# Two-stream diffusion step: the entering states of the backward scan copied by ScalarE in all four groups, not by GpSimd in three

## The reference, cut to what matters

```python
bu = einsum("blgc,gpc->blgp", u, b_bar)          # real and imaginary part
h[l] = a_bar * h[l-1] + bu[l]                    # forward, and on the reversed tokens
y = einsum(h_fwd, c_fwd) + einsum(h_bwd, c_bwd)[reversed] + d_skip * u
y = gelu(y); y = y * sigmoid(y @ w_glu + b_glu)
out = (y * silu(z)) @ w_out ;  x = x + gate * out
```

## Time and profile before

| | us |
|---|---|
| median of 3 runs (lowest, highest) | 1102.53 (1101.49, 1105.61) |
| time of the profiled execution | 1102.69 |
| its span | 1100.9 |
| granted clock of TensorE, mean | 0.992 |
| TensorE matmuls busy | 1054.0 (96%) |
| VectorE busy | 766.8 (70%) |
| ScalarE busy | 538.3 (49%) |
| GpSimd busy | 227.3 (21%) |
| all 284 grouped low-part subtractions (L1557) | 347.9 |
| all 284 grouped high-part roundings (L1152) | 299.2 |

### The profile page before, as it was taken

How to read it: one execution, slowest core, us unless ns; L and a number is a source line. 1 busy time by engine, 2 the same in 40 slices (tenths; PEclk the granted TensorE clock), 3 DMA queues, 4 the chain that set the end, 5 groups by cost and what they waited for, 6 DMA issues and landing times.

```text
span 1100.9 us, 18580 instructions
## 1 busy us (share of the span) xinstructions
PE 1054.0 (96%) x7426; PEld 823.8 (75%) x7426; DVE 766.8 (70%) x1206; ACT 538.3 (49%) x759; POOL 227.3 (21%) x382
## 2 busy tenths in 40 slices
PE   3999999999999999999999989999999989999996
PEld 2777777777777777777777768888788868878885
DVE  2765686766577667766688876369998996476564
ACT  5334454444434344444444465566657466454442
POOL 1111230432043403321233340200222322100000
PEclk9999999999999999999999999999999999999999
DMA  9999978999789979997799987968684958865552
GB/s 378 419 419 419 380 285 317 359 347 350 289 318 356 361 276 344 340 354 262 286 369 348 349 317 261 286 220 251 185 268 156 297 186 290 299 237 173 187 197 93
DMA packets 62407, 325.61 MB, mean 296 GB/s; under 512 B 8209, under 2 KB 14993, under 8 KB 30193
## 3 DMA queue, kind: packets, MB, share of 16 engines
q1 hardware_dynamic: 42944, 267.93, 65.4%
q0 software_dynamic: 12176, 45.33, 11.9%
q10 hardware_dynamic: 7200, 11.16, 2.8%
HBM read 296.04 MB, written 28.34 MB: 295 GB/s over the span
## 4 chain that ended last, share of the span: by engine, by line
PE 75%; DVE 10%; DMA 7%; ACT 4%; issue 2%; SPq 0%; POOL 0%; ACTq 0%; DVEq 0%
PE ps L867 20%; PE ps L869 19%; PE ps L868 19%; DMA raw<-in_w 5%; PE ps L732 5%; DVE wlo L1557 3%; DMA early<-in_wada 2%; DVE sb L1685 2%; PE ps L991 2%; PE ps L806 1%; ACT whi L1152 1%; PE ps L1015 1%; PE ps L789 1%; DVE t L1680 1%; PE ps L751 1%
## 5 line engine op out<-in xcount | busy, mean ns | idle before, releaser
L1557 DVE TENSOR_TENSOR wlo<-raw,whi 128x1024 fp32r<-128x1024 f32 x284 | 347.9, 1228 | 232.6 <-ACT whi L1152 227.8
L1152 ACT ACTIVATE whi<-raw 128x1024 fp32r<-128x1024 f32 x284 | 299.2, 1058 | 397.6 <-PE ps L869 373.5
L867 PE MATMUL ps<-whi,xhi 128*128 128x512 f32 x1136 | 460.5, 405 | 9.7 <-DVE wlo L1557 6.6
L868 PE MATMUL ps<-wlo,xhi 128*128 128x512 f32 x1152 | 451.2, 392 | 0.0
L869 PE MATMUL ps<-whi,xlo 128*128 128x512 f32 x1136 | 445.2, 392 | 0.0
L867 PEld LDWEIGHTS ps<-whi,xhi 128*128 128x128 f32 x1136 | 214.1, 188 | 83.7 <-issue 18.9
L869 PEld LDWEIGHTS ps<-whi,xlo 128*128 128x128 f32 x1136 | 214.1, 188 | 47.2
L868 PEld LDWEIGHTS ps<-wlo,xhi 128*128 128x128 f32 x1152 | 217.5, 189 | 41.0
L732 PE MATMUL ps<-araw,cT 128*32 128x512 f32 x496 | 59.4, 596 | 0.0
L1685 DVE TENSOR_TENSOR sb<-sb,t 128x128 f32<-128x128 f32 x140 | 48.4, 349 | 4.6
L1575 DVE TENSOR_TENSOR xlo<-ps,xhi 128x512 fp32r<-128x512 f32 x40 | 27.5, 689 | 16.9 <-ACT xhi L1173 16.6
(11 more groups left out here) (236 smaller groups left out, 1066.2 us busy)
## 6 DMA issues: line engine op xcount, KB each, us to landing
raw<-in_w SPq DMA_DIRECT2D x144, 1024.0 KB, 7.0
araw<-in_wadag SPq DMA_DIRECT2D x62, 1024.0 KB, 9.0
early<-in_wada SPq DMA_DIRECT2D x20, 1024.0 KB, 19.0
araw<-in_wada SPq DMA_DIRECT2D x12, 1024.0 KB, 17.6
btab_scratch<-bs ACTq DMA_DIRECT2D x32, 256.0 KB, 6.2
ctab_scratch<-ce POOLq DMA_DIRECT2D x16, 512.0 KB, 8.6
btab<-btab_scratch SPq DMA_DIRECT2D x16, 512.0 KB, 4.6
ctab<-ctab_scratch POOLq DMA_DIRECT2D x16, 512.0 KB, 4.7
```

Of the source, the lines that this page charges most:

```text
L867: mm(acc, xhi[:, kt, st], hi[:, k], start=kt == 0, stop=False)
L868: mm(acc, xhi[:, kt, st], wlo[:, slot, k0 % 2, k], start=False, stop=False)
L1152: af(whi_at(k).rearrange("p k c -> p (k c)"), src, ACT.Copy).then_inc(s_hi, 1)
L1557: tt(wlo[:, slot, k % 2].rearrange("p k c -> p (k c)"), src, whi_at(k).rearrange("p k c -> p (k c)").bitcast(F32), ALU.subtract).then_inc( ...
```

## The change

For the groups 0, 1 and 2 the backward half of the entering states is copied by ScalarE, as it already is for group 3. GpSimd's function goes, with its waits, and so does the semaphore `s_hyb` that TensorE, ScalarE and GpSimd waited for.

```diff
-            def entering_backward(w):
-                pool.wait_ge(s_scan, w + 1)
-                if w == 0:
-                    pool.wait_ge(s_h0, 16)
-                for q in range(4):
-                    if (w, q) == (0, 2):
-                        pool.wait_ge(s_uT, 2 * NW)
-                        pool.wait_ge(s_u2p, 2 * NW)
-                    if w >= 1:
-                        pool.wait_ge(s_y, 4 * w + q - 3)
-                    pool.wait_ge(s_wused, HY_AT[w] + q + 1)
-                    dst, first, src = entering(w, q)
-                    nc.gpsimd.tensor_copy(dst[S5P:P, :, :, NCH - 1], first[S5P:P])
-                    nc.gpsimd.tensor_copy(dst[S5P:P, :, :, 0:NCH - 1], src[S5P:P, :, :, ::-1]).then_inc(s_hyb, 1)
...
-            entering_backward(0)
-            entering_backward(1)
-            entering_backward(2)
-            pool.wait_ge(s_hyb, 12)
...
                 pe.wait_ge(s_hy, n + 1)
-                pe.wait_ge(s_hyb, min(n + 1, 4 * (NW - 1)))
...
                     act.wait_ge(s_hy, 4 * (w - 2) + q + 1)
-                    act.wait_ge(s_hyb, 4 * (w - 2) + q + 1)
...
                 af(fwd[:, :, :, 0], first[0:S5P], ACT.Copy)
-                if w == NW - 1:
-                    af(bwd[:, :, :, NCH - 1], first[S5P:P], ACT.Copy)
-                    nc.scalar.copy(bwd[:, :, :, 0:NCH - 1], src[S5P:P, :, :, ::-1])
+                if n == 0:
+                    act.wait_ge(s_h0, 16)
+                af(bwd[:, :, :, NCH - 1], first[S5P:P], ACT.Copy)
+                nc.scalar.copy(bwd[:, :, :, 0:NCH - 1], src[S5P:P, :, :, ::-1])
                 nc.scalar.copy(fwd[:, :, :, 1:NCH], src[0:S5P]).then_inc(s_hy, 1)
```

More of the change, by code:

```diff
@@ L389, in build @@
         s_S, s_Ssb = sem("S_pe"), sem("S_sb")
-        s_scan, s_hy, s_hyb, s_y, s_ysb = sem("scan"), sem("hy"), sem("hy_backward"), sem("y_pe"), sem("y_sb")
+        s_scan, s_hy, s_y, s_ysb = sem("scan"), sem("hy"), sem("y_pe"), sem("y_sb")
         s_yout, s_yin = sem("y_stored"), [sem(f"y_in{i}") for i in range(NW)]
```

## The result

The changed kernel takes 1106.74 us in the median of 20 runs (1104.47 to 1114.73), the kernel before 1102.49: 4.3 us slower by the medians. The ratio of the means is 1.0043, with a 95% interval of 1.0034 to 1.0051, or +4.7 us; a run of the kernel before that took 1184.40 us is not in it. That is clearly slower, and not quite the 0.5% that the prediction took as the line for a change. Forecast were 1104.5 us and "the same". The profiled execution of the changed kernel is its fastest one: 1104.47 us, span 1102.2, against 1102.69 and 1100.9 of the one before. Of the 4.3 us it shows only 1.8.

A forecast was written before the change was run, and what follows sets the result against it. TensorE, busy 96%, was taken to bound the kernel, with ScalarE and VectorE as possible limits beside it. Delays less VectorE's gain came to +1.8, taken as +2.0 us: 1104.7 on the profiled execution, 1104.5 forecast, range 1102 to 1107.

The forecast's parts named there:

- GpSimd's side costs nothing: Removing twelve pairs of GpSimd copies gains nothing directly, as the loads queued behind them wait for other things anyway: 0 us.
- VectorE gets 8.8 us back: VectorE's instructions, no longer lengthened by GpSimd's copies, give back 3.1, 2.3 and 3.4 us in groups 0, 1 and 2.
- ScalarE's price: Each added pair of copies costs ScalarE 1.38 us a quarter, 16.6 us in all, with ends of 1.1 and 1.4.
- ScalarE, group 0: Four extra pairs delay TensorE's sums at 793.64 by 2.45 us, group 2's scan by 5.0, the outputs at 805.08 by 3.4.
- the rival of the clock: TensorE's clock falls in new waits near 796 and 842, 1.6 us each: 1105.2 us, 1106.8 with another at 891; chance 0.28.
- ScalarE, group 1: Extra pairs, partly absorbed by ScalarE's waits, delay group 3's scan by 6.1 us and TensorE's sums near 838 by 4.8.
- VectorE, group 2: VectorE starts 6.1 us late, gets 3.4 back: TensorE +2.7 at 891.25, then +1.1 without the clock's fall; 905.91 at +1.8.
- The sum: The +1.8 us at TensorE's outputs at 905.91 reaches the end of the kernel; taken as +2.0 with TensorE's new waits.
- the allowance: TensorE's new waits, over 2 us each, may add up to 1 us; the total was raised from +1.8 to +2.0.
- ScalarE has no room in groups 0 and 1: Denies the rival that the extra pairs vanish in ScalarE's waits, leaving 4.3 us gained: 1098.2 us, chance 0.12.
- VectorE's time would not come back: Rival: ScalarE's copies lengthen VectorE's additions too, so +6.1 us at group 3's scan reaches the end: 1108.6 to 1111, chance 0.15.

The follow-up runs named there:

- the run in which both engines copy: The changed kernel with GpSimd still copying the same states of groups 0 to 2 into unread spare memory: 1108.23 us, ratio 1.0051 against the kernel before.
- group 2 alone: The kernel before with only group 2's backward half moved to ScalarE: 1099.60 us, ratio 0.9976 against the kernel before.

## Why the prediction was right, and where it was short

*GpSimd's side costs nothing.* Right: TensorE names no table load among its waits.

*VectorE gets 8.8 us back.* Right: its busy time fell by 9.4 us on the page of the profile, 8.0 of them in the additions, and L1663 is at 292 ns throughout. The 0.7 us that were not in the sum are one low-part subtraction at 837.58, in group 1, which a copy lengthened as well (1962 ns where the median is 1226):

```profile
L1557 DVE TENSOR_TENSOR wlo<-raw,whi x26: 1212/1226/1962, 782.6 to 890.0; 128x1024 fp32r<-128x1024 f32 x26
```

The rule of the Trainium skill (SBUF — State Buffer, "SBUF: two separate sides"), an exclusive lock between VectorE and GpSimd, agrees in kind with the run in which both engines copy: its additions reach 686 ns, and 294 without GpSimd's copies. What a pair of copies cost VectorE here was 9.4 / 12 = 0.8 us, less than the 1.22 us of the long one alone. The prediction had the same 0.8, though its own sum of 8.8 us gives 0.7.

*ScalarE's price.* Its busy time rose by 14.7 us for twelve pairs, 1.2 us a pair and not 1.38, inside the ends of 1.1 and 1.4. That is why the delays of group 0 came out somewhat smaller than forecast.

*ScalarE, group 0.* Forecast +2.45, +5.0 and +3.4 us at the sums, the scan and the second outputs; the rows give 795.69 - 793.64 = +2.05, 810.32 - 805.97 = +4.35 and 808.69 - 805.08 = +3.6. The last one came by another way than in my sum: no wait for the GELU is in the row, since the clock had fallen meanwhile and TensorE came late by itself, as the rival of the clock has it. In the second profile of the changed kernel, without that fall, TensorE does wait for the GELU there, and the delay is 808.16 - 805.08 = +3.1:

```profile
808.16 0.68 PE L989 MATMUL ps<-kd,utf 64*64 64x64 f32 x16 [0.85 <-ACT ys L1255]
```

*ScalarE, group 1.* Forecast +6.1 at the scan and +4.8 at the sums; the rows give 854.81 - 848.90 = +5.9 and 842.57 - 837.68 = +4.9.

*VectorE, group 2.* Forecast +2.7 and a wait of 0.4 us; the rows give 893.73 - 891.25 = +2.5 and 0.34. The outputs after it: +1.1 forecast, 896.67 - 895.79 = +0.9 measured. That the clock doesn't fall there any more was right. At the GELU near 906: +1.8 forecast, 907.13 - 905.91 = +1.2 measured.

*The sum.* It was +1.8 before the allowance. The profiled execution is 1.8 us above the profiled one of before in time and 1.3 in span, with +1.2 at the last of these rows, so the equal 1.8 is in part luck. The median is 4.3 above. The term that was mis-sized is the allowance for the new waits of TensorE: "may add up to 1", of which 0.2 went into the forecast. Keeping TensorE busy in these waits took off 2.4 us. That the median still lies inside the stated range, 1102 to 1107, is owed to the range's upper half, which was kept for one more fall of the clock.

I had this mechanism as a rival with a chance of 0.28 and weighed it too low, although both new waits came out at 2 us in my own sum, the length behind which the clock had fallen before. Its prices for one fall hold in the traces: 1.6 us behind the second wait, and next to nothing behind the first. Its total of 1105.2 is still 1.5 us below the median, and its upper end of 1106.8 needed a third fall at 891, which neither profile of the changed kernel shows; that the median comes near that end is luck. The clock falls behind one new wait in each of the two profiles, and not the same one, and behind both in the run in which both engines copy (0.69 from 796, 0.50 from 845). A single profile can therefore miss this cost, as the first one, of the fastest run, does.

*The rivals.* ScalarE has no room in groups 0 and 1 (4.1 and 3.3 us alone). It has room in group 2, and there the change alone is a gain. That VectorE's time would not come back is refuted by L1663's 294 ns at most beside two long ScalarE copies a quarter, and by group 2 alone.

## What to carry to other kernels

When work moves between helper engines, price it stage by stage at the wait that it stands before: here four pairs cost 4.1 us in one stage and gained 2.6 in another, and the right change was to move one group of three. In the stage where ScalarE showed no idle time, four added pairs of 1.2 us put the scan 4.35 us later, so they were paid nearly in full, and what VectorE gained there was lost waiting for ScalarE. A new wait of TensorE can cost more than its length, as the clock may fall behind it (1.6 us here); compare it with the waits behind which the trace shows a fall, and take the price against the median of several runs, not against one profile.

## What the runs showed of the hardware that I had not expected

Sixteen idle transposes put into each of two waits of about 2 us made the kernel 2.4 us faster in the median. Its 11 runs lie within 1.2 us, the five of the changed kernel beside them within 2.4 (1104.92 to 1107.29). And with GpSimd's copy cut in two, of 0.75 and 0.66 us, and written to other memory, the longest lengthened addition was 686 ns and not 1232; which of the two differences did it was not tried apart.
